# Prompt's attention output and new state from shared stationary v tiles, in rounded products with split rests

## The reference, cut to what matters

```python
q_t = qb * jnp.exp(b)
k_t = kb * jnp.exp(-b)
att = jnp.where(mask, jnp.einsum('bhtd,bhsd->bhts', q_t, k_t), 0.0)
o = jnp.einsum('bhts,bhsv->bhtv', att, vb) + jnp.einsum('bhtd,bhdv->bhtv', q_t, S)
...
k_d = kb * jnp.exp(b_last - b)
S = jnp.exp(b_last[..., 0, :])[..., None] * S + jnp.einsum('bhsd,bhsv->bhdv', k_d, vb)
```

## Time and profile before

| | us |
|---|---|
| median of 3 runs | 957.65 |
| lowest, highest | 957.04, 958.0 |
| the profiled execution, span | 955.9 |
| TensorE busy in it | 951.2 |
| VectorE, ScalarE, GpSimd busy | 559.5, 374.6, 106.8 |

### The profile page before, as it was taken

One profiled execution on the slowest core, in us unless ns is written; L12 is line 12 of the kernel. 1 busy time (PEld: TensorE's weight loads), 2 busy tenths in 40 slices (PEclk: granted clock), 3 DMA queues, 4 the chain that ended last, 5 costly groups with the idle time before them and its releaser, 6 DMA issues.

```text
span 955.9 us, 17387 instructions
## 1 busy us (share of the span) xinstructions
PE 951.2 (100%) x6666; PEld 942.8 (99%) x6666; DVE 559.5 (59%) x776; ACT 374.6 (39%) x467; POOL 106.8 (11%) x103
## 2 busy tenths in 40 slices
PE   9999999999999999999999999999999999999998
PEld 9999999999999999999999999999999999999998
DVE  6948778737795576444444444444455444597443
ACT  7545244232253444333333333333333333455331
POOL 0000001112244640000000000000002333100000
PEclk9999999999999999999999999999999999999999
DMA  9535445977654454444444444444447444346541
GB/s 344 186 132 177 141 129 185 221 250 249 221 177 137 160 168 141 155 154 151 143 147 152 154 137 155 146 154 154 143 146 275 154 151 144 122 133 226 175 154 39
DMA packets 56159, 159.65 MB, mean 167 GB/s; under 512 B 6452, under 2 KB 19896, under 8 KB 56120
## 3 DMA queue, kind: packets, MB, share of 16 engines
q1 hardware_dynamic: 42640, 143.18, 46.1%
q10 hardware_dynamic: 13480, 15.93, 4.9%
HBM read 149.91 MB, written 9.18 MB: 166 GB/s over the span
## 4 chain that ended last, share of the span: by engine, by line
PE 100%; DVE 0%; POOL 0%; issue 0%; DVEq 0%; POOLq 0%
PE bank L1282 30%; PE bank L1284 29%; PE bank L1283 29%; PE bank L1344 1%; PE bank L1347 1%; PE bank L1563 1%; PE bank L1353 1%; PE bank L1560 1%; PE bank L1557 1%; PE bank L1315 0%; PE bank L1313 0%; PE bank L1314 0%; PE bank L1320 0%; PE bank L1504 0%; PE bank L1443 0%; PE bank L1454 0%
## 5 line engine op out<-in xcount | busy, mean ns | idle before, releaser
L713 DVE TENSOR_TENSOR w_lo<-w_raw,w_hi 128x1024 fp32r<-128x1024 f32 x252 | 314.4, 1253 | 332.8 <-ACT w_hi L607 166.0
L1282 PE MATMUL bank<-x_hi,w_hi 128*128 128x320 f32 x1216 | 377.0, 310 | 0.0
L1284 PE MATMUL bank<-x_hi,w_lo 128*128 128x320 f32 x1216 | 375.7, 309 | 0.0
L1283 PE MATMUL bank<-x_lo,w_hi 128*128 128x320 f32 x1216 | 375.7, 309 | 0.0
L404 ACT ACTIVATE w_hi<-w_raw 128x1024 fp32r<-128x1024 f32 x148 | 156.0, 1058 | 260.8 <-PE bank L1284 244.5
L1282 PEld LDWEIGHTS bank<-x_hi,w_hi 128*128 128x128 f32 x1216 | 228.2, 188 | 2.0 <-issue 1.8
L1283 PEld LDWEIGHTS bank<-x_lo,w_hi 128*128 128x128 f32 x1216 | 228.3, 188 | 0.0
L1284 PEld LDWEIGHTS bank<-x_hi,w_lo 128*128 128x128 f32 x1216 | 228.2, 188 | 0.0
L607 ACT ACTIVATE w_hi<-w_raw 128x1024 fp32r<-128x1024 f32 x96 | 101.6, 1058 | 115.8 <-PE bank L1284 115.8
L1282 PE MATMUL bank<-m_hi,w_hi 128*128 128x320 f32 x448 | 138.4, 309 | 0.0
L1283 PE MATMUL bank<-m_lo,w_hi 128*128 128x320 f32 x448 | 138.4, 309 | 0.0
(11 more groups left out here) (247 smaller groups left out, 902.0 us busy)
## 6 DMA issues: line engine op xcount, KB each, us to landing
w_raw<-in_w_units SPq DMA_DIRECT2D x258, 512.0 KB, 3.4
state_dec<-in_s ACTq DMA_DIRECT2D x8, 512.0 KB, 6.9
out_st_dec<-state_dec ACTq DMA_DIRECT2D x8, 512.0 KB, 5.7
h<-in_x_t ACTq DMA_DIRECT2D x4, 640.0 KB, 7.9
out_y<-pe_out ACTq DMA_DIRECT2D x16, 160.0 KB, 2.5
x_sb<-in_x_t SPq DMA_DIRECT2D x6, 320.0 KB, 7.8
v_rows<-v_parts SPq DMA_DIRECT2D x4, 256.0 KB
v_stacked_rows<-v_rows SPq DMA_DIRECT2D x4, 256.0 KB, 7.8
```

What stands on the lines that cost most here:

```text
L713: dve.tensor_tensor(wlo[:, q], raw[:, q], whi[:, q].bitcast(F32), ALU.subtract).then_inc(lo_ready, 1)
L1282: pe.matmul(acc, h, hi[:, k0 + k, :], start=first and k == 0, stop=False)
L1283: pe.matmul(acc, h, lo[:, k0 + k, :], start=False, stop=False)
L1284: m = pe.matmul(acc, l, hi[:, k0 + k, :], start=False, stop=last and k == UK - 1)
```

## The change

- `o_prompt` and the state's matmuls become one function, `o_and_state(i)`, run for 8 tiles of v (128 channels each) after z7. Its stationary side is a tile of v; its moving side is attention (256 columns, or 128 for the second half of the tokens) with decayed k (128 columns) behind it in one tile, `ak`. All go in the rounded type in three products, so 6 matmuls a tile: 3 of 384 and 3 of 256 columns. The block after va0 is gone. Each tile has a bank of its own (`OP_BANKS`).
- v, attention and decayed k are therefore split too: ScalarE rounds them (`round_v`, `round_att_and_kd`), in 6 new instructions, and GpSimd makes the 6 rests (`split_v`, `split_att_and_kd`). GpSimd also makes the two rests of the new tokens' v and k that VectorE made.
- VectorE's transposes are dealt out anew: eight in each of z2 to z6 (v, k, k, v, v), where before it were 4, 7, 7, 6 of v in z2 to z5 and all 16 of k in z6.
- ScalarE copies out 256 and 128 columns for each of the 8 tiles. The state is kept with v's channels on the partitions, stored so, and turned outside the device.
- `v_hi` and a part of `ak_hi` lie where the stacked rows go, so `load_rows` now waits for the last of the 8 tiles. Only the first old state is loaded after z7; three more follow after the copies.

```diff
-        VT_STEPS = {S_V + 5: (0, 4), S_V + 7: (4, 2), S_ZB: (6, 2), S_ZB + 2: (8, 4), S_ZB + 3: (12, 7), S_ZB + 4: (19, 7),
-                    S_ZB + 5: (26, 6)}
+        VT_STEPS = {S_V + 5: (0, 4), S_V + 7: (4, 2), S_ZB: (6, 2), S_ZB + 2: (8, 8), S_ZB + 5: (16, 8), S_ZB + 6: (24, 8)}
+        KT_STEPS = {S_ZB + 3: (0, 8), S_ZB + 4: (8, 8)}
@@ sync
-                if 4 <= n < 4 + HB:
-                    sp.wait_ge(rows_stored, 16 * 8)
-                    load_rows(n - 4)
+            sp.wait_ge(rows_stored, 16 * 8)
+            sp.wait_ge(op_done, KE)
+            for h in range(HB):
+                load_rows(h)
@@ scalar
+            def copy_o_and_state(i):
+
+                act.wait_ge(op_done, i + 1)
+                act.activation(o_sb[:, i, 0:SEQ], bank[OP_BANKS[i]][:, 0:SEQ], ACT.Copy).then_inc(op_copied, 1)
+                act.activation(st[:, i, :], bank[OP_BANKS[i]][:, SEQ:SEQ + DK], ACT.Copy).then_inc(op_copied, 1)
...
+            def round_v(n):
+                act.wait_ge(vt_ready, 16 * (n + 1))
+                act.activation(v_hi[:, :, 512 * n:512 * n + 512], v_t[:, :, 512 * n:512 * n + 512], ACT.Copy).then_inc(vp_hi, 1)
...
-                split_hi(s)
+                split_hi(s, halves=(0,))
+                if t == 7:
+                    round_v(1)
+                split_hi(s, halves=(1,))
                 sigmoid(s)
...
+                if t == 1:
+                    act.wait_ge(att_masked, 3)
+                    act.wait_ge(att_copied, 7)
+                    round_att_and_kd(0, SEQ)
+                if t == 3:
+                    round_v(0)
+                if t == 5:
+                    act.wait_ge(kdt_ready, 4 * (P // BLK))
+                    round_att_and_kd(SEQ, SEQ + DK)
                 if t == 7:
-                    act.wait_ge(kdt_ready, 4 * (P // BLK))
-                    for b in range(3):
-                        load_s0(b)
+                    act.wait_ge(rows_stored, 16 * 8)
+                    load_s0(0)
@@ vector
-                if t == 2:
-                    for n, (parts, x) in enumerate(((v_parts, v_ts), (k_parts, k_ts))):
-                        dve.wait_ge(parts_hi, n + 1)
-                        dve.tensor_tensor(parts[:, 1, :], x[:], parts[:, 0, :].bitcast(F32), ALU.subtract)\
-                           .then_inc(parts_lo, 1)
@@ gpsimd
             for t in range(KE):
+                if t == 7:
+                    split_v(1)
                 gate(t, zb_gate[:, t, :])
...
+                if t == 2:
+                    split_att_and_kd(0, 0, SEQ)
+                    for n, (parts, x) in enumerate(((v_parts, v_ts), (k_parts, k_ts))):
+                        pool.wait_ge(parts_hi, n + 1)
+                        pool.tensor_tensor(parts[:, 1, :], x[:], parts[:, 0, :].bitcast(F32), ALU.subtract)\
+                            .then_inc(parts_lo, 1)
+                if t == 3:
+                    split_v(0)
+                if t == 5:
+                    split_att_and_kd(2, SEQ, SEQ + DK)
@@ tensor
+            def o_and_state(i):
+
+                h, dv = i // 2, slice(P * i, P * i + P)
+                for c in range(2):
+                    acc = bank[OP_BANKS[i]][:, P * c:SEQ + DK]
+                    x_hi, x_lo = ak_hi[c][:, h, :], ak_lo[:, c, h, P * c:SEQ + DK]
+                    pe.matmul(acc, v_hi[:, c, dv], x_hi, start=c == 0, stop=False, skip_group_check=True)
+                    pe.matmul(acc, v_hi[:, c, dv], x_lo, start=False, stop=False, skip_group_check=True)
+                    m = pe.matmul(acc, v_lo[:, c, dv], x_hi, start=False, stop=c == 1, skip_group_check=True)
                 m.then_inc(op_done, 1)
...
                 if t == 7:
-                    pe.wait_ge(att_masked, 3)
-                    pe.wait_ge(att_copied, 7)
-                    pe.wait_ge(vt_ready, 4 * SEQ // BLK)
-                    for n in range(2):
-                        o_prompt(n)
+                    pe.wait_ge(ak_split, 4)
+                    pe.wait_ge(acc_read, S_VA - 1)
+                    for i in range(KE):
+                        if i % 4 == 0:
+                            pe.wait_ge(vp_lo, i // 4 + 1)
+                        if i == KE - 1:
+                            pe.wait_ge(acc_read, S_VA)
+                        o_and_state(i)
...
             for c, s in enumerate(range(S_VA, S_ZA)):
+                if c < 2:
+                    pe.wait_ge(op_copied, 2 * KE if c else 2)
                 step(s, xhi, xlo)
-                if c == 0:
-
-                    pe.wait_ge(kdt_ready, 4 * (P // BLK))
-                    for h in range(HB):
-                        for c2 in range(2):
-                            m = pe.matmul(bank[4 + h // 2][:, DV * (h % 2):DV * (h % 2) + DV],
-                                          kd_t[:, c2, DK * h:DK * h + DK], v_t[:, c2, DV * h:DV * h + DV],
-                                          start=c2 == 0, stop=c2 == 1)
-                    m.then_inc(ps_done, 1)
```

More of the change, by code:

```diff
@@ L469, in sigmoid @@
                 sig_t.up(act.activation(sig[:, s % 2, :], tmp[:, s % 2, :], ACT.Sigmoid))
-            def copy_banks(dst, banks, rows, done):
-                for c, b in enumerate(banks):
-                    act.activation(dst[:, 512 * c:512 * c + 512], bank[b][0:rows, :], ACT.Copy).then_inc(done, 1)
             def load_s0(b):
@@ L954, in _ @@
                     dve.wait_ge(att_done, 1)
-                    for c, dst in enumerate((att0, att1)):
+                    for c in range(2):
                         for g in range(4):
```

115 lines of the change are left out of this document (60 added, 55 removed).

## The result

| | before | after |
|---|---|---|
| median of 5 runs | 957.48 us | 961.74 us |
| lowest, highest | 956.92, 958.00 | 960.45, 962.58 |
| span of the profiled execution | 955.9 us | 960.9 us |

The ratio is 1.0043, 95% interval 1.0031 to 1.0056. The forecast was 957.7 us in a range of 955.4 to 960.0. The profiled execution of after is the longest of its five; the spans of the others are 958.7 to 960.2.

A forecast was written before the change was run, and what follows sets the result against it. TensorE's own stream was taken as the bound (busy 951.2 of 955.9 us, full clock). Removed 8.82, added 7.04 and a new wait of 1.8 sum to 0.0, giving 957.7 us on the median 957.65; range 955.4 to 960.0.

The forecast's parts named there:

- SyncE's queue: Stacked-row loads start at 191.2 instead of 173.8, land in 4 to 8 us, cover 2 us or more, cost 0.
- The stacked rows come late: Rival: last row load needs 14.0 us, TensorE stands 3.8 us before sequences(0), 961.5 us in all; chance 0.13.
- Rounded matmuls: TensorE's eight tiles: 48 rounded matmuls at a mean of 320 columns, 146.7 ns each, 7.04 us (bounds 6.40 to 7.74).
- the gap rule: Skill page's N / 2.4 + 2.5 ns per matmul, not followed: the 48 would cost 6.52 us, net -2.30.
- Removed 8.82: TensorE loses the separate blocks of o_prompt, 5.37 us, and of the state, 3.45 us: together 8.82 us.
- the ledger: GpSimd and VectorE through z2 to z7: backlog makes v's second rest late (187.7), so TensorE waits 1.8 us at the fifth tile.
- GpSimd's rest of 1024 columns: GpSimd's two-operand rest of 1024 columns in the z steps takes 2.40 us, bounds 2.05 and 2.82.
- in turns, as read: GpSimd operations and VectorE ones reading two SBUF operands run one after the other; transposes and results out of PSUM are untouched.
- the roundings on ScalarE: Six ScalarE roundings, five before z7 in idle time, 1.06 us per 1024 columns: hidden.
- the freed VectorE: VectorE loses two rests and the 7.43 us run of 16 transposes, which nobody waited for: no gain.

The follow-up runs named there:

- states_only_later: Changed kernel with only old states b = 2, 3 and 5 moved behind the roundings of va1, the state's store left in place: 957.02 us, ratio 0.9996.
- states_later: Changed kernel with old states b = 2, 3 and 5 and the state's store issued behind the roundings of va1: 956.57 us, ratio 0.9993.
- apart_only: Changed kernel with stacked-row loads of heads 2 and 3 issued by ScalarE ahead of old states b = 1 to 3, nothing else moved: 956.81 us, ratio 0.9994.
- rows_early: Changed kernel with memory laid out anew so nothing covers the stacked rows, which SyncE loads at their old place in z5 and z6: 956.66 us, ratio 0.9993.
- store_later: Changed kernel with the state's store and old state b = 5 moved behind the roundings of va1, b = 1 to 3 left in place: 962.23 us, ratio 1.0056.
- quarters: rows_early with the roundings and rests of v's two halves each cut in two, each pair of tiles waiting for its quarter: 955.79 us, ratio 0.9985.
- stand: rows_early with a TensorE stand of about 3 us after va1, made by GpSimd writing zeros three times, not by a transfer: 963.01 us, ratio 1.0054.
- before_late: Kernel before with its stacked-row loads held until ScalarE has copied the first two banks of o_prompt: 964.84 us, ratio 1.0075.
- its two relatives: Kernel before with rows held likewise, and old states b = 1, 2, 3, 5 (964.55 us) or only b = 2, 3, 5 (958.31 us) moved behind va1's roundings.
- one_state: Changed kernel with old states b = 1, 2, 3 and 5 and the state's store all behind the roundings of va1: 962.91 us, ratio 1.0058.
- before_late_states01: Kernel before with rows held as in before_late and old states b = 2, 3 and 5 moved behind the roundings of va1: median 958.31 us, ratio 1.0014.

## Why the prediction was wrong

**The step that failed is "SyncE's queue".** It took the landing as 4 to 8 us, "after the change no weights stand between them", and so a cover of 2 us or more and a cost of 0. Measured: the last k row in up to 12.6 us. Two things were missed. The old states b = 1 to 3, issued at 190.5 to 191.5 on ScalarE's queue, share the DMA engines with the rows; the step names them as late, yet only asks when they are wanted themselves, not whom they hold up. With b = 2 and 3 out of the way the rows landed in 8.1 (states_only_later) and 9.5 us (states_later). And the rows are slow without any company: 1.57 MB at 205 to 213 GB/s is 7.5 us of full DMA engines before anything else has its turn. The first of these numbers could have been read in before: while its rows moved, 184 to 190 us, the stretches show 201 to 217 GB/s with the engines full:

```profile
184.00:186.00 2.00, 2.00 (x21) 2.00 (x20) 1.87 (x5) 0.00 (x0) 0.00 (x0) 1.00 1.19 202
186.00:188.00 2.00, 2.00 (x20) 2.00 (x19) 2.00 (x2) 0.00 (x0) 0.00 (x0) 1.00 0.98 201
188.00:190.00 2.00, 2.00 (x16) 2.00 (x15) 0.50 (x2) 0.47 (x1) 0.88 (x1) 1.00 1.18 217
```

From 190.5 the engines had to bring 1.57 MB of rows and 1.57 MB of three old states besides the rest of a fourth, 3.1 MB and more; at the 237 to 279 GB/s of 192 to 202 us in after that is 11 to 13 us plus the start, against 14.08 of cover. Cost zero was a guess at the favourable end. The sum shows that the cover was thin, not that it had to fail: by 204.4 the engines of the changed kernel had brought 3.9 MB (280 GB/s from 190.5 on) and not yet all the rows, with the store, b = 5 and the weights issued from 197.0 under way as well, while apart_only's brought 4.3 MB by 204.1 (313 GB/s) with its rows there at 200.3. Which transfer is served when counts beside how many bytes there are.

**The rival had it.** "The stacked rows come late" names the place, the releaser, and for its reason "three old states and the state's store start in the same window". It gave 961.5 us, the median is 961.74. The agreement is partly luck: its 3.8 us of stand measured 2.8, and it has no price for the clock, 1.5 to 3.0 us. Of its two reasons the store turned out to count for nothing. It had a chance of 0.13, since "the high values belong to a queue full of weights". They do not: rows_early's k rows, between weights, took up to 12.0, after's, with no weights between them, 12.6. The range ended at 960.0 and left this case out by intent.

**The clock had no term.** The text reads a full clock in all 40 slices and prices every wait at its length. A wait of about 1 us does cost its length: at the tiles (1.0 to 1.1) the clock stayed full. The 2.8 us at the rows cost about twice theirs in the profiled execution; the stand of 3.4 in store_later cost 1.5 on top.

**What held.** Rounded matmuls: 24 pairs of 384 and 256 columns start every 0.177 and 0.118 us (181.91 to 185.33 and on), so 24 x 0.295 = 7.08 us; forecast 7.04 by keeping the mean pitch, and by the gap rule 6.52. That rule (the Trainium skill, TensorE: Matmul & The Clock Gate, section Back-to-back issue gap) is 9 to 14 ns short at both widths, as at 320 columns (11). The section gives it for an isolated matmul and says that in a stream of weight loads and matmuls both set the spacing, which the prediction left out. Removed 8.82, added 7.08 and a wait of 1.31 (8.39 for the block, 181.91 to 190.30): net -0.43, forecast 0.0.

The wait came from where the ledger has it, only smaller, 1.3 for 1.8. Rows of VectorE and GpSimd in after, the places of the ledger:

```profile
160.98 4.77 DVE L733 TENSOR_TENSOR w_lo<-w_raw,w_hi 128x1024 fp32r<-128x1024 f32 x2
165.68 0.48 DVE L958 TENSOR_TENSOR tmp<-bank,r_tok 128x320 f32<-128x320 f32 x1
...
179.33 3.72 DVE L928 STREAM_TRANSPOSE v_tokens<-v_b 32x256 f32<-32x256 f32 x8
...
161.27 3.39 POOL L1243 TENSOR_TENSOR v_tokens_lo<-v_tokens,v_tokens_hi 128x1024 fp32r<-128x1024 f32 x1
...
184.22 2.38 POOL L1243 TENSOR_TENSOR v_tokens_lo<-v_tokens,v_tokens_hi 128x1024 fp32r<-128x1024 f32 x1 [3.46 <-ACT v_tokens_hi L485]
```

Alone, GpSimd's rest of 1024 columns takes 2.38 (forecast 2.40). Beside VectorE's rests it takes 3.39, and VectorE's two rests 4.77 instead of 2.36: in turns, as read. The scaled result of z4 is at 165.68 (forecast 166.7; before 163.79, and all is 0.5 earlier), v's second half complete at 183.05 (forecast 184.1), its rest at 186.60 (forecast 187.7). Once the early start of 0.5 is taken off, the ledger is 0.5 us later than measured from z4 on and carries that to the end: the 0.5 by which the wait is smaller. quarters shows the rest of the mechanism: ready by quarters, v keeps TensorE waiting not at all, and that is worth 0.9 us (956.66 to 955.79).

Neither the roundings on ScalarE nor the freed VectorE showed as a wait of TensorE or a gain, as forecast.

## What to carry to other kernels

When a change moves a transfer later, its cover must be held at least against the time in which the DMA engines bring all that is then under way on every queue, at the rate that the trace shows for this very transfer, which was little more than half of what others reached here. A stand of TensorE of about 3 us cost one and a half times to twice its length here, so a wait that may reach that size needs a case of its own and not a place in the tail. And loads into 32 neighbouring partitions moved a quarter faster here when they were under way together with ones for the other half of the partitions, on two queues; done ahead of the old states, that took the whole loss away (apart_only).

## What the chip did that I had not expected

- A stand of 2.8 to 5.1 us (after, stand, before_late and its two relatives, store_later, one_state) brought the granted clock to 0.50 each time, by whatever releaser, and it stayed there for some microseconds of full work, in two lengths: 6.8 us in after (207.2 to 214.0) and about as long in stand (208.3 to 215.1), 3.4 in store_later (209.1 to 212.6). Spread over the execution these make a mean clock of 0.996 and 0.998; four of after's five executions have 0.998, so I put them down to the shorter, without a profile of them. Twenty throw-away matmuls in the gap kept it at 1.00. The stands of 1.0 and 1.1 us at the tiles did not touch it.
- 32-partition loads alone fill the DMA engines at 205 to 213 GB/s; paired across the halves of the partitions 267 to 278, paired within a half 214 to 227.
- A transfer of 0.5 MB out of SBUF (the state's store), queued behind the old states, cost the rows nothing, 1 MB of loads (b = 2 and 3) beside them 3 to 4.5 us.
- The same arrangement (before_late_states01) took 957.3 to 960.0 us in eight executions, and 963.2 and 964.7 in two, the profiled one of which stood 4.0 us for its rows; the cause of that scatter stays open.
